# A two-block model on one core: the mixer's residual added by tokens and turned once, rope halves swapped by transfers, identity transposes in two waits

## The reference: what is computed

```python
h = rmsnorm_2(x, norm_mix_pre)
proj = h @ w_in
# differential attention: dq, dk by 4 x 2 heads of 64, both through rope
out = concatenate([x1 * cos - x2 * sin, x2 * cos + x1 * sin])   # rope: x1, x2 are halves of a head
...
mixed = jnp.concatenate([o_diff, o_mlstm], axis=-1) @ w_out
x = x + rmsnorm_2(mixed, norm_mix_post)
h = rmsnorm_2(x, norm_mlp_pre)
u = jnp.square(jax.nn.relu(h @ w_up))
x = x + rmsnorm_2(u @ w_down, norm_mlp_post)
```

## Time and profile before

| what | value |
| --- | --- |
| median of 3 runs | 1560.13 us (1559.62 to 1560.41) |
| profiled execution, its time | 1560.29 us |
| its span, first to last instruction | 1558.3 us |
| TensorE busy | 1535.7 us (99%), weight loads 1241.9 |
| VectorE, ScalarE, GpSimd busy | 739.8, 559.6, 80.2 us |
| mean granted TensorE clock | 0.999 |
| moved by transfers | 149.08 MB, mean 96 GB/s |

### The profile page before, as it was taken

The page is one execution under the profiler, slowest core; times in us unless marked ns, Lnnn a source line. Parts: engine busy times, 40 slices in busy tenths (PEclk is TensorE's granted clock), DMA queues, the critical chain, the costliest instruction groups (busy, mean ns, idle before and its releaser), DMA issues.

```text
span 1558.3 us, 19012 instructions
## 1 busy us (share of the span) xinstructions
PE 1535.7 (99%) x7098; PEld 1241.9 (80%) x7098; DVE 739.8 (47%) x1068; ACT 559.6 (36%) x909; POOL 80.2 (5%) x66
## 2 busy tenths in 40 slices
PE   8999999999999999999999999999999999999998
PEld 6888888887875788888888878766789888888886
DVE  5444422346346654444323474575554643234434
ACT  5322221234225542322212273355644433124322
POOL 0000000002013210000000051100000000000000
PEclk9999999999999999999999999999999999999999
DMA  6333353334221233333333333421132332233222
GB/s 182 99 102 96 94 136 94 99 103 121 82 74 40 76 101 98 100 98 94 95 94 96 101 102 95 121 57 54 53 127 77 95 94 95 95 99 101 97 95 95
DMA packets 246296, 149.08 MB, mean 96 GB/s; under 512 B 17616, under 2 KB 230240, under 8 KB 245984
## 3 DMA queue, kind: packets, MB, share of 16 engines
q1 hardware_dynamic: 232896, 141.58, 30.8%
q10 hardware_dynamic: 13344, 6.75, 1.7%
HBM read 144.10 MB, written 5.78 MB: 96 GB/s over the span
## 4 chain that ended last, share of the span: by engine, by line
PE 94%; DVE 3%; ACT 2%; issue 1%; DMA 0%; POOL 0%; SPq 0%; DVEq 0%; ACTq 0%; POOLq 0%
PE bank L348 29%; PE bank L352 29%; PE bank L351 28%; DVE w_low L1110 1%; PE bank L2021 1%; PE bank L2073 1%; PE bank L2250 1%; PE bank L2032 1%; DMA region_f<-in_x 0%; PE bank L2366 0%; PE bank L2363 0%; PE bank L2196 0%; PE bank L2155 0%; PE bank L1960 0%; PE bank L2105 0%
## 5 line engine op out<-in xcount | busy, mean ns | idle before, releaser
L348 PE MATMUL bank<-region,w_high 128*128 128x512 f32 (+2 forms) x1492 | 586.3, 393 | 3.9 <-DVE w_low L1110 1.7
L352 PE MATMUL bank<-region,w_low 128*128 128x512 f32 (+2 forms) x1492 | 580.1, 389 | 0.0
L351 PE MATMUL bank<-region,w_high 128*128 128x512 f32 (+2 forms) x1492 | 579.7, 389 | 0.0
L1110 DVE TENSOR_TENSOR w_low<-w_raw,w_high 128x1024 fp32r<-128x1024 f32 (+1 forms) x259 | 334.8, 1299 | 143.8 <-ACT w_high L598 140.1
L598 ACT CAST w_high<-w_raw 128x1024 fp32r<-128x1024 f32 (+1 forms) x259 | 265.6, 1027 | 264.2 <-DMA w_raw<-in_ffn_w_down 107.5
L348 PEld LDWEIGHTS bank<-region,w_high 128*128 128x128 f32 (+1 forms) x1492 | 280.2, 188 | 66.6 <-DVE w_low L1110 4.3
L352 PEld LDWEIGHTS bank<-region,w_low 128*128 128x128 f32 (+1 forms) x1492 | 279.9, 188 | 59.5
L351 PEld LDWEIGHTS bank<-region,w_high 128*128 128x128 f32 (+1 forms) x1492 | 280.1, 188 | 56.1
L348 PE MATMUL bank<-w_high,region 128*128 128x512 f32 x416 | 164.5, 395 | 2.3 <-DVE w_low L1110 1.4
L352 PE MATMUL bank<-w_high,region 128*128 128x512 f32 x416 | 162.2, 390 | 0.0
L351 PE MATMUL bank<-w_low,region 128*128 128x512 f32 x416 | 161.9, 389 | 0.0
(11 more groups left out here) (255 smaller groups left out, 1095.1 us busy)
## 6 DMA issues: line engine op xcount, KB each, us to landing
w_raw<-in_ffn_w_down SPq DMA_DIRECT2D x48, 512.0 KB, 3.9
w_raw<-in_ffn_w_gate SPq DMA_DIRECT2D x44, 512.0 KB, 3.8
w_raw<-in_ffn_w_up SPq DMA_DIRECT2D x44, 512.0 KB, 3.8
w_raw<-in_w_in SPq DMA_DIRECT2D x40, 512.0 KB, 3.9
w_raw<-in_w_up SPq DMA_DIRECT2D x32, 512.0 KB, 4.0
w_raw<-in_w_down SPq DMA_DIRECT2D x32, 512.0 KB, 3.3
w_raw<-in_w_out SPq DMA_DIRECT2D x16, 512.0 KB, 3.9
region_f<-in_x SPq DMA_DIRECT2D x4, 512.0 KB, 7.6
```

The costliest lines, as they stand in the source:

```text
L348: mm = pe.matmul(out, a_hi, b_hi, start=start, stop=False)
L351: pe.matmul(out, a_hi, b_lo, start=False, stop=False)
L352: return pe.matmul(out, a_lo, b_hi, start=False, stop=stop)
L1110: last = dve.tensor_tensor(piece(w_low[b % RING]), piece(w_raw[b % RING]), piece(w_high[b % RING]).bitcast(F32), ALU.subtract)
```

## The change

Four edits in three places of the program.

1. **Rope.** `swap_halves` moves from TensorE to SyncE. For each column four transfers of 32 partitions by 512 copy `rope_y` into `rope_w` with halves exchanged, SBUF to SBUF. They wait for `rope_y` to be written and, from the third on, for the rope sum two columns back. They stand in SyncE's queue behind the fetch of a weight block four columns on, the last four behind the fetches of `dv`. VectorE's product reads `rope_w` instead of PSUM and writes it in place.
2. **Mixer.** VectorE adds the residual by tokens before the turn: in `mix_scale` a `scalar_tensor_tensor` over 128 x 1024 takes the place of `mix_ident`, and `x_add` is gone. `turn_mixed` waits for that and turns the sum with eight transposes. Banks are 2 and 3 for group 0, 4 and 5 for groups 1 and 3, 6 and 7 for group 2. The order on ScalarE and VectorE changes with it: the square and sum of groups 2 and 3 stand behind the parts of groups 0 and 1.
3. **m2.** 12 transposes of the identity into bank 7, which nobody reads, ahead of `norm_stat`.
4. **Start.** 10 transposes of the identity into bank 1 ahead of x, and 14 more behind the second tile.

```diff
+            def swap_halves(i):
+
+                sp.wait_ge(acc_free, RES["dqk"] + i + 1)
+                if i >= 2:
+                    sp.wait_ge(r_full, i - 1)
+                for p0 in range(0, P, 32):
+                    p1 = p0 ^ 32
+                    sp.dma_start(rope_w[p0:p0 + 32, i % 2, :], rope_y[p1:p1 + 32, i % 4, :]).then_inc(r_perm[i % 2], 16)
+
+            for j in range(8):
+                fetch(sp, BLK["dqk"] + j, w_dram["w_in_2"][:, :, j * P:(j + 1) * P])
+                if j >= 4:
+                    swap_halves(j - 4)
+            for j in range(4):
+                fetch(sp, BLK["dv"] + j, w_dram["w_in_2"][:, 2 * j:2 * j + 2, 1024:1024 + S], width=S)
+                swap_halves(4 + j)
...
@@ VectorE, rope @@
-                dve.wait_ge(r_perm, i + 1)
-                link(dve.tensor_tensor(rope_s[:, i % 2, :], bank[6 + i % 2][:], const[:, C_SIN:C_SIN + S], ALU.mult))
+                dve.wait_ge(r_perm[i % 2], 64 * (i // 2 + 1))
+                link(dve.tensor_tensor(rope_w[:, i % 2, :], rope_w[:, i % 2, :], const[:, C_SIN:C_SIN + S], ALU.mult))
...
@@ VectorE, mixer @@
-                if t_ >= 2:
-                    dve.wait_ge(p_turned, t_ - 1)
-                dve.tensor_scalar(mix_ident[:, t_ % 2, :], CI(C_IDENT), mix_r[:, t_:t_ + 1], None, ALU.mult).then_inc(p_ident, 1)
+                dve.wait_ge(x_returned[t_], 16)
+                dve.scalar_tensor_tensor(x_rows[:, t_, :], mixed[:, t_, :], mix_r[:, t_:t_ + 1], x_rows[:, t_, :],
+                                         ALU.mult, ALU.add).then_inc(x_new, 1)
...
-            mix_lo(0)
             split_lo(BLK["f3_up0"])
-            mix_lo(1)
+            for t_ in range(2):
+                mix_lo(t_)
+                mix_scale(2 + t_)
+            split_lo(BLK["f3_up0"] + 1)
             for t_ in range(2, TT):
-                mix_scale(t_)
-            mix_lo(2)
-            split_lo(BLK["f3_up0"] + 1)
-            mix_lo(3)
+                mix_lo(t_)
...
@@ ScalarE, mixer @@
-            mix_hi(0)
             split_hi(BLK["f3_up0"])
-            mix_hi(1)
-            mix_square(1, 2)
-            mix_deviation(2)
-            mix_square(1, 3)
-            mix_deviation(3)
-            mix_hi(2)
+            for t_ in range(2):
+                mix_hi(t_)
+                mix_square(1, 2 + t_)
+                mix_deviation(2 + t_)
             split_hi(BLK["f3_up0"] + 1)
-            mix_hi(3)
+            for t_ in range(2, TT):
+                mix_hi(t_)
...
@@ TensorE, start @@
+            def keep_busy(n, out):
+
+                for _ in range(n):
+                    pe.transpose(out[:, 0:P], CI(C_IDENT), CI(C_IDENT))
+
             pe.wait_ge(ident_in, 16)
+            keep_busy(10, bank[1])
             for n in range(DT):
+                if n == 2:
+                    keep_busy(14, bank[1])
...
@@ TensorE, m2 @@
+            keep_busy(12, bank[7])
             norm_stat("m2", 2)
...
@@ TensorE, mixer @@
-                pe.wait_ge(x_returned[t_], 16)
+                pe.wait_ge(x_new, X_NEW["post"] + t_ + 1)
                 if t_ == 0:
                     pe.wait_ge(acc_free, RES["out2"] + TT)
-                if t_ >= 2:
-                    pe.wait_ge(xt_lo, GEN["f3"] + DT * (t_ - 1))
+                if t_ == 2:
+                    pe.wait_ge(acc_free, RES["out2"] + TT + 2)
+                if t_ == 3:
+                    pe.wait_ge(xt_lo, GEN["f3"] + DT * 2)
                 for n in range(DT):
-                    pe.matmul(where(n), x_rows[:, t_, n * P:(n + 1) * P], CI(C_IDENT), start=n % 4 == 0, stop=False)
-                pe.wait_ge(p_ident, t_ + 1)
-                for n in range(DT):
-                    mm = pe.matmul(where(n), mixed[:, t_, n * P:(n + 1) * P], mix_ident[:, t_ % 2, :], start=False, stop=n % 4 == 3)
+                    mm = pe.transpose(turn_bank(t_, n), x_rows[:, t_, n * P:(n + 1) * P], CI(C_IDENT))
                 mm.then_inc(p_turned, 1)
...
-            up_half(1, 0, {0: turned_by(2, DT - 1)})
+            up_half(1, 0, {})
```

More of the change, by code:

```diff
@@ L228, in build @@
                 rope_c = sb("rope_c", [P, 2, S], F32, s2)
-                rope_s = sb("rope_s", [P, 2, S], F32, s2)
+                rope_w = sb("rope_w", [P, 2, S], F32, s2)
             with ExitStack() as s2:
@@ L260, in x_bank, with turn_bank @@
             return bank[2 + n % 6]
+        def turn_bank(t, n):
+            return bank[(2, 4, 6, 4)[t] + n // 4][:, n % 4 * P:(n % 4 + 1) * P]
         def f3_half(t, c):
@@ L333, in build @@
         token_sq, token_std = sem("token_squares_ready"), sem("token_std_ready")
-        p_ident, p_turned = sem("mix_scaled_identity_ready"), sem("mix_x_turned")
+        p_turned = sem("x_turned_back")
         q_ready, o_sum = sem("token_columns_ready"), sem("out_summed")
@@ L465, in build @@
         tables_scaled = sem("rope_tables_scaled")
-        r_perm, r_cos = sem("rope_swapped"), sem("rope_cos_ready")
+        r_perm, r_cos = [sem("rope_swapped0"), sem("rope_swapped1")], sem("rope_cos_ready")
         r_full = sem("rope_ready")
@@ L1024, in mix_hi @@
                         act.wait_ge(xt_lo, GEN["f3"] + DT * t_ + i - 1)
-                    act.activation(f3_in(n)[0][:, t_ * P:(t_ + 1) * P], bank[2 * (1 + t_ % 2) + n // 4][:, n % 4 * P:(n % 4 + 1) * P],
+                    act.activation(f3_in(n)[0][:, t_ * P:(t_ + 1) * P], turn_bank(t_, n),
                                    ACT.Identity, scale=gains[:, 5, n:n + 1]).then_inc(xt_hi, 1)
@@ L1437, in rope_sum @@
             def rope_sum(i):
-                dve.wait_ge(r_perm, i + 1)
-                link(dve.tensor_tensor(rope_s[:, i % 2, :], bank[6 + i % 2][:], const[:, C_SIN:C_SIN + S], ALU.mult))
+                dve.wait_ge(r_perm[i % 2], 64 * (i // 2 + 1))
+                link(dve.tensor_tensor(rope_w[:, i % 2, :], rope_w[:, i % 2, :], const[:, C_SIN:C_SIN + S], ALU.mult))
                 dve.wait_ge(r_cos, i + 1)
-                dve.tensor_tensor(over[1][:, i, :], rope_c[:, i % 2, :], rope_s[:, i % 2, :], ALU.add).then_inc(r_full, 1)
+                dve.tensor_tensor(over[1][:, i, :], rope_c[:, i % 2, :], rope_w[:, i % 2, :], ALU.add).then_inc(r_full, 1)
             for i in range(8):
@@ L1694, in f3_acc @@
                 return f3_bank(c, t_)
-            for t_ in range(TT):
-                x_add(t_)
             up("f3_up0", part[0], False, lambda: None)
@@ L2175, in after_dv @@
             def after_dv(j):
-                for i in ((5, ), (6,), (7,), (), (), (), (), ())[j]:
-                    swap_halves(i)
                 if j < 2:
```

12 lines of the change are left out of this document (1 added, 11 removed).

## The result

| what | before | changed |
| --- | --- | --- |
| median | 1559.88 us (1559.49 to 1560.41, 4 executions) | 1540.24 us (1540.18 to 1540.38, 4 executions) |
| ratio | | 0.9873, 95% interval 0.9859 to 0.9888 |
| span of the profiled execution | 1558.3 us | 1538.4 us |
| TensorE busy | 1535.7 us | 1520.2 us |

What follows compares the result with a forecast made beforehand. TensorE, holding 94% of the chain and hardly waiting, was taken to bound the kernel. Savings of 1.1 + 1.6 + 6.9 + 9.6 = 19.2 us off the profiled 1560.29 gave a forecast of 1541.0 us, range 1538.4 to 1546.5.

Steps and rivals of the forecast that it cites:

- Start: Program start: transpose fills bring the fast clock early, first matmul at 13.3 to 13.4 instead of 14.46; 1.1 us saved.
- m2: Wait for POOL ahead of the second block's statistics: 12 fills keep the clock from falling and delay nothing; 1.6 us saved.
- Rope: Rope stage: eight swaps of 0.86 us leave TensorE, which never waits there, and the transfers are covered; 6.9 us saved.
- Mixer: Mixer's end: eight transposes replace 16 exact matmuls per group, less a new 2.1 us wait for low parts; 9.6 us saved.
- rival 2: Mixer gives back more or weights come late behind swaps: 9.6 becomes 5, 6.9 becomes 5; 1547.5 us; chance 0.12.
- Rival 1: Clock does not follow the fills, or falls in the mixer's new wait: 1543.7, or 1545.4 with that fall; chance 0.20.
- Rival 4: Rope: swaps choke the SyncE queue and the kernel gets slower, if swap landings exceed 14.3 us; chance 0.03.
- Rival 3: Rope and mixer: matmul slots are hidden anyway by other engines, so no change, 1558 to 1562 us; chance 0.03.

Runs made afterwards that it cites:

- by-bank run: Against the changed kernel, ScalarE rounds a group's eight slices bank by bank in the last FFN, VectorE starting once four are rounded: 1538.58 us.
- by-bank run with the earlier split: Low parts bank by bank, plus the weight split of the third FFN's first block one group earlier, against the changed kernel: 1539.64 us.

## Why the prediction was right

1541.0 was forecast and 1540.24 measured. The sum was 19.2 us; the traces give 19.9.

- **Start, 1.1 forecast, 1.5 in the trace.** The landing of the last quarter of x was put at 12.4; TensorE's wait for it ends at 12.08, which is 0.3 of the difference. The claim on which the term rests, that the clock rises on transposes alone, holds: with fills the first two matmuls are 0.32 us apart and the next 0.23, without them 0.46 and 0.23. Taking the fills out costs 1.65 us in the traced execution and 0.9 in the median, so the forecast's 1.1 lies between the two. The rule of the Trainium skill, "TensorE: Matmul & The Clock Gate", Part 4 (PE-mode transpose), under which both fills are useless, is contradicted by these rows.
- **m2, 1.6 forecast.** The traces of before and changed differ by 1.56 us here, and the median without the fills is 1.3 us up. That the fills are the cause at this place is not shown: without them one execution kept its clock here and lost it at 1048. The prediction took the fall for a fixed cost of this wait. At this wait and at the one at 1048 it comes in some executions and not in others. That 1.6 came out so well is in part luck: the one trace that the term was read from is one in which the clock fell here.
- **Rope, 6.9 forecast, 6.9 in the trace, 6.5 by taking it back.** The slot was right. Two sizes beside it were off and cost nothing: an issue is 0.6 us and not 0.37, and a swap lands in 3.5 and not 5. A column is 5.93 and not 5.8, of which 24 slots of 0.227 leave 0.48 for the turns between columns, not 0.35.
- **Mixer, 9.6 forecast, 10.0 in the trace.** The new wait was foreseen at its place, 1.34 us instead of 2.1, a turn is 0.79 us instead of 0.70, and the wait at the third block went. From the first turn to the third block the forecast had 23.2 us (1181.82 to 1205.0), the trace 22.87. The wait was shorter mainly because TensorE came to it 0.5 us later, 8.7 us behind the first turn and not 8.3, and VectorE was done 0.2 us sooner. The last 0.4 us come from the halves behind the last turn: they ran through in 8.82 us (1185.89 to 1194.71), where the forecast let them follow the low parts of groups 2 and 3 for 9.2. The alternation of the two engines that rival 2 named is the wait's cause (by-bank run), but its price was far from the 4.6 us that rival 2 put on the mixer.
- **Rival 1** had the right fact, that a fill needn't hold a clock, at the wrong place: neither m2 nor the mixer's new wait fell, and the wait at 1048, which no step of the prediction looked at, did in other kernels.
- **Rival 4** is real: with 16 transfers a swap the kernel is slower than before. Its threshold was in the wrong quantity. It counted the landing (8.7 us to grow a column, 14.3 to lose); what grew was SyncE's issue time, and the column's 5.93 us is its limit. The changed kernel uses 2.8 to 3.5 us of that with its fetch; twice as many transfers fill it.
- **Rival 3** (the slots are hidden anyway) is refuted by the rope and the mixer put back, which cost 6.5 and 10.1 us, nearly their slots in full.

## What to carry to other kernels

Where one engine holds 94% of the chain and waits for almost nothing, an instruction taken off it is worth its slot, and what to check is the engine that takes over: for a DMA queue, issues per step times the issue's own time against the length of the step, since landings overlap and issues don't. Where two engines hand slices to each other one by one, let each do a bank's worth before it signals; here that took a new wait away at no cost. Waits of over a microsecond on TensorE are worth removing twice, for their length and for the clock that sometimes falls behind them, and such a fall can come at one place in one execution and at another in the next, so compare several executions before a fill gets the credit.

## What the runs showed of the hardware

- Transposes alone raise TensorE's clock. When it rises varies: the fourteen fills at the start took 7.31 to 9.53 in the changed kernel, 0.16 us each, and 7.55 to 10.53 in the kernel with the swaps put back, 0.21 us each, where all 24 turns behind them then ran at 0.115 without a wait. In the by-bank run they took 6.45 to 8.14, 0.12 us each.
- A fall of the granted clock to 0.50 cost 1.6 us behind m2's statistics before the change and 1.1 to 1.3 us at 1048 (the run without m2's fills, the by-bank run with the earlier split), and it comes in some executions only. Behind the same 1.45 us wait at 1048 the clock stayed at 1.00 in the traces of the changed kernel and fell in those of two others, out of twelve traces that have it. The executions of a kernel that sometimes falls spread by 1.3 us (1.29 without m2's fills, 1.35 in the by-bank run with the earlier split), against 0.43 in the changed kernel. With that wait removed they spread by 0.78 us in one kernel and 0.36 in the other, so the wait is not all that varies.
- A copy of 32 partitions of 2 KB from SBUF to SBUF takes SyncE's queue 0.59 us to issue (median), one of 16 partitions 0.59 and one of 8 partitions 0.62, while 512 KB from DRAM take 0.37, and 0.44 to 0.58 directly behind such copies. The cost is per transfer and does not fall with its size. A copy of 32 partitions lands in 2.0 to 5.5 us.
